# The first microseconds of an encoder kernel: x in column halves, the first weight tile in blocks

## The reference, cut to what matters

```python
def _rmsnorm(x, g):
    y = xf * lax.rsqrt(jnp.mean(xf * xf, axis=-1, keepdims=True) + RMS_EPS)
    return (y * g.astype(jnp.float32)).astype(x.dtype)

def _pool_mixer(h, w_in, w_group, scale, w_out):
    u = (h @ w_in).reshape(b, s, N_POOL_GROUPS, POOL_GROUP)      # h, w_in: 256x1024, 1024x1024
    ...                                                          # pooling, grouped product
    return y @ w_out

def reference(x, ...):
    for i in range(DEPTH):                    # DEPTH = 2
        hn = _rmsnorm(x, norm_mix[i])
        y = _pool_mixer(hn, ...)  if mixer == 0 else _dilated_mixer(hn, ...)
        x = x + y
        hn = _rmsnorm(x, norm_ffn[i])
        x = x + (_swiglu(hn, ...) if i % 2 == 0 else _moe(hn, ...))   # d_ff 3584; top 2 of 8 experts
    return _rmsnorm(x, norm_final)
```

## Time and profile before

| | |
|---|---|
| median of three runs | 1650.28 us |
| profiled execution, its own time | 1648.55 us |
| its span, first to last instruction | 1646.7 us |
| PE busy | 1595.2 us, 97% of the span |
| DVE, ACT busy | 1193.8 us (72%), 1006.1 us (61%) |
| chain that ended last | PE 93%, DVE 3%, issue 2%, ACT 1% |
| first matmul of the product starts | 15.41 us |
| first matmul with tile 1 starts | 21.08 us |

### The profile page before, as it was taken

How to read it: one execution, slowest core, us unless ns; L and a number is a source line. 1 busy time by engine, 2 the same in 40 slices (tenths; PEclk the granted TensorE clock), 3 DMA queues, 4 the chain that set the end, 5 groups by cost and what they waited for, 6 DMA issues and landing times.

```text
span 1646.7 us, 21670 instructions
## 1 busy us (share of the span) xinstructions
PE 1595.2 (97%) x7925; PEld 1311.0 (80%) x7925; DVE 1193.8 (72%) x977; ACT 1006.1 (61%) x815; POOL 130.3 (8%) x127
## 2 busy tenths in 40 slices
PE   8999999999899998999999999999999999995996
PEld 6888888899799876888888888888888888884885
DVE  4555454454654568888888888888888888984886
ACT  5444443433633466777777777777777777774774
POOL 0000000050332222000000000000000000000000
PEclk9999999999999999999999999999999999997998
DMA  9555555476266417999999999999999999997992
GB/s 344 187 181 180 192 182 184 154 240 196 77 188 221 154 53 268 360 375 356 372 377 353 375 374 353 375 371 356 376 372 355 370 378 355 376 345 252 364 360 86
DMA packets 237712, 468.87 MB, mean 285 GB/s; under 512 B 9632, under 2 KB 15776, under 8 KB 237648
## 3 DMA queue, kind: packets, MB, share of 16 engines
q1 hardware_dynamic: 231216, 454.06, 78.8%
q0 software_dynamic: 3024, 11.01, 2.2%
q10 hardware_dynamic: 3408, 2.93, 0.6%
HBM read 460.60 MB, written 7.37 MB: 284 GB/s over the span
## 4 chain that ended last, share of the span: by engine, by line
PE 93%; DVE 3%; issue 2%; ACT 1%; DMA 0%; SPq 0%; ACTq 0%; DVEq 0%
PE bY L291 9%; PE bY L293 9%; PE bY L292 9%; PE bU L291 8%; PE bG L291 8%; PE bU L293 8%; PE bU L292 8%; PE bG L292 8%; PE bG L293 8%; PE bS L293 3%; PE bS L292 3%; PE bS L291 3%; PE bT L530 2%; DVE logit L1238 1%; PE bT L293 1%
## 5 line engine op out<-in xcount | busy, mean ns | idle before, releaser
L281 DVE TENSOR_TENSOR wlo<-raw,whi 128x2048 fp32r<-128x2048 f32 x427 | 978.4, 2294 | 367.6 <-ACT whi L275 366.4
L275 ACT ACTIVATE whi<-raw 128x2048 fp32r<-128x2048 f32 x427 | 818.8, 1918 | 472.8 <-PE bY L293 163.7
L291 PE MATMUL bG<-whi,eTh 128*128 128x512 f32 x448 | 179.5, 401 | 16.9 <-issue 16.9
L291 PE MATMUL bU<-whi,eTh 128*128 128x512 f32 x448 | 182.9, 408 | 4.9 <-DVE wlo L281 4.9
L291 PE MATMUL bY<-whi,hTh 128*128 128x512 f32 x448 | 178.9, 399 | 0.0
L292 PE MATMUL bG<-whi,eTl 128*128 128x512 f32 x448 | 178.3, 398 | 0.0
L293 PE MATMUL bG<-wlo,eTh 128*128 128x512 f32 x448 | 178.2, 398 | 0.0
L292 PE MATMUL bU<-whi,eTl 128*128 128x512 f32 x448 | 178.1, 398 | 0.0
L293 PE MATMUL bU<-wlo,eTh 128*128 128x512 f32 x448 | 178.0, 397 | 0.0
L292 PE MATMUL bY<-whi,hTl 128*128 128x512 f32 x448 | 177.6, 396 | 0.0
L293 PE MATMUL bY<-wlo,hTh 128*128 128x512 f32 x448 | 177.5, 396 | 0.0
(11 more groups left out here) (404 smaller groups left out, 2333.9 us busy)
## 6 DMA issues: line engine op xcount, KB each, us to landing
raw<-in_m_w_gate_up_dram SPq DMA_DIRECT2D x224, 1024.0 KB, 6.4
raw<-in_m_w_down_dram SPq DMA_DIRECT2D x112, 1024.0 KB, 6.4
raw<-in_b_w_in_dram SPq DMA_DIRECT2D x36, 1024.0 KB, 5.2
raw<-in_f_w_gate_up_dram SPq DMA_DIRECT2D x28, 1024.0 KB, 5.2
raw<-in_f_w_down_dram SPq DMA_DIRECT2D x14, 1024.0 KB, 5.1
raw<-in_a_w_in_dram SPq DMA_DIRECT2D x4, 1024.0 KB, 11.2
raw<-in_a_w_out_dram SPq DMA_DIRECT2D x4, 1024.0 KB, 15.7
biasrev<-toeplitz SPq DMA_DIRECT2D x32, 128.0 KB, 4.9
```

The costliest lines, as they stand in the source:

```text
L275: nc.scalar.activation(whi[:, t % CUT], raw[:, t % RAW], ACT.Copy).then_inc(hi_done, 1)
L281: nc.vector.tensor_tensor(wlo[:, t % CUT], raw[:, t % RAW], whi[:, t % CUT].bitcast(F32), ALU.subtract).then_inc(lo_done, 1)
L291: pe.matmul(dst, a[0], b[0], start=start, stop=False)
```

## The change

x is loaded by halves of its columns: seven DMAs of 128 KB on SP and one on ACT's queue (`load_x`), with a semaphore for each half. The first weight tile is loaded as four DMAs of 128 rows (256 KB, a block each), between the two halves of x. ACT and DVE make its high and low parts block by block (128x512), with `first_hi` and `first_lo` counting. On PE 16 spare matmuls stand ahead of the transposes instead of 14, 6 behind instead of 15; the transposes of the second half of x stand between blocks 1 and 2 of tile 0; and tile 0 is worked by block (G and U in turn) instead of by bank. ACT and DVE make the high and low parts of tile 1 ahead of `xTh` and `xTl` of x's second half. ACT's table load waits for the zeroed tile instead of for the gains.

```diff
+        def load_x(engine, a, kh):
+            sl = slice(kh * 512, kh * 512 + 512)
+            engine.dma_start(x[a % 2 * 64:a % 2 * 64 + 64, a // 2, sl],
+                             x_in[0].rearrange("(m a) d -> a m d", a=4)[a][:, sl]).then_inc(x_in_done[kh], 16)
...
         @block.sync
         def _(sp):
+            for a in range(3):
+                load_x(sp, a, 0)
+            for b in range(4):
+                sp.dma_start(raw[:, 0, b * 512:b * 512 + 512],
+                             tile_source(0)[b * P:b * P + P, :]).then_inc(first_full[b], 16)
             for a in range(4):
-                sp.dma_start(x[a % 2 * 64:a % 2 * 64 + 64, a // 2, :],
-                             x_in[0].rearrange("(m a) d -> a m d", a=4)[a]).then_inc(x_in_done, 16)
+                load_x(sp, a, 1)
...
-            for t in range(T_MOE + CUT):
+            for t in range(1, T_MOE + CUT):
                 load(t)
...
             pe.wait_ge(spare_zero, 2)
-            spare(14, yTh[:, 0, 0:P], mixTh[:, 0:2])
+            spare(16, yTh[:, 0, 0:P], mixTh[:, 0:2])
             pe.wait_ge(c_in[C_IDENT], 16)
             turn_x(0, 0)
-            turn_x(0, 1)
-            spare(5, yTh[:, 0, 0:P], mixTh[:, 0:2])
-            spare(5, yTh[:, 1, P:2 * P], mixTh[:, 2:4])
-            spare(5, mixTh[:, 0, 0:P], mixTh[:, 2:4])
+            spare(6, yTh[:, 0, 0:P], mixTh[:, 0:2])
             pe.wait_ge(tx_lo, 2)
-            dense(T_IN, xTh, xTl, KH, (G, U), [lambda: pe.wait_ge(tx_lo, 4)])
+            for b in range(4):
+                pe.wait_ge(*((first_lo, b + 1) if b < 3 else (lo_done, 1)))
+                for tb, bank in enumerate((G, U)):
+                    mm = mm3(pe, bank[:], tok(xTh, xTl, b, tb), wblk(0, b), start=b == 0, stop=False)
+                if b == 1:
+                    turn_x(0, 1)
+            mm.then_inc(tile_used, 1)
+            pe.wait_ge(tx_lo, 4)
+            tile_ready(1)
...
             load_const((C_IDENT, C_GAINT))
+            load_x(act, 3, 0)
+            act.wait_ge(spare_zero, 2)
+            nc.scalar.activation(small[:, 8:9], yTh[:, 0, 0:1].bitcast(F32), ACT.Copy)
             act.wait_ge(c_in[C_IDENT], 16)
             act.wait_ge(c_in[C_GAINT], 16)
-            nc.scalar.activation(small[:, 8:9], gainT[:, 0, 0:1], ACT.Copy)
             cut_x(0, 0)
             load_const((C_BUCKET, C_RELB, C_SCALE))
-            make_hi(act, 0)
+            for b in range(4):
+                act.wait_ge(first_full[b], 16)
+                sl = slice(b * 512, b * 512 + 512)
+                nc.scalar.activation(whi[:, 0, sl], raw[:, 0, sl], ACT.Copy).then_inc(*((first_hi, 1) if b < 3 else (hi_done, 1)))
+            make_hi(act, 1)
             cut_x(0, 1)
-            for t in range(1, CUT):
-                make_hi(act, t)
+            make_hi(act, 2)
...
             cut_x(0, 0)
-            make_lo(dve, 0)
+            for b in range(4):
+                dve.wait_ge(*((first_hi, b + 1) if b < 3 else (hi_done, 1)))
+                sl = slice(b * 512, b * 512 + 512)
+                nc.vector.tensor_tensor(wlo[:, 0, sl], raw[:, 0, sl], whi[:, 0, sl].bitcast(F32),
+                                        ALU.subtract).then_inc(*((first_lo, 1) if b < 3 else (lo_done, 1)))
+            make_lo(dve, 1)
             cut_x(0, 1)
-            for t in range(1, CUT):
-                make_lo(dve, t)
+            make_lo(dve, 2)
```

More of the change, by code:

```diff
@@ L192, in encoder @@
         acc_dram = nc.dram_tensor("summed", (S + P, D), F32, kind="Internal").ap()
-        x_in_done = sem("x_in_done")
+        x_in_done = [sem("x_in_done0"), sem("x_in_done1")]
+        first_full, first_hi, first_lo = [sem(f"first_full{b}") for b in range(4)], sem("first_hi"), sem("first_lo")
         spare_zero = sem("spare_zero")
@@ L268, in tile_source @@
             return ffn_tile(m_w_gate_up[0, 0], m_w_down[0, 0], t - T_MOE)
+        def load_x(engine, a, kh):
+            sl = slice(kh * 512, kh * 512 + 512)
+            engine.dma_start(x[a % 2 * 64:a % 2 * 64 + 64, a // 2, sl],
+                             x_in[0].rearrange("(m a) d -> a m d", a=4)[a][:, sl]).then_inc(x_in_done[kh], 16)
         def make_hi(act, t, item=0):
-            act.wait_ge(raw_full[t % RAW], item * (16 * (FFN_TILES // RAW)) + 16 * (t // RAW + 1))
+            act.wait_ge(raw_full[t % RAW], item * (16 * (FFN_TILES // RAW)) + 16 * ((t - 1) // RAW + 1))
             if t >= CUT:
@@ L446, in turn_x @@
                 if n == 0:
-                    pe.wait_ge(x_in_done, 64)
+                    pe.wait_ge(x_in_done[kh], 64)
                 else:
@@ L482, in _ @@
             pe.wait_ge(spare_zero, 2)
-            spare(14, yTh[:, 0, 0:P], mixTh[:, 0:2])
+            spare(16, yTh[:, 0, 0:P], mixTh[:, 0:2])
             pe.wait_ge(c_in[C_IDENT], 16)
             turn_x(0, 0)
-            turn_x(0, 1)
-            spare(5, yTh[:, 0, 0:P], mixTh[:, 0:2])
-            spare(5, yTh[:, 1, P:2 * P], mixTh[:, 2:4])
-            spare(5, mixTh[:, 0, 0:P], mixTh[:, 2:4])
+            spare(6, yTh[:, 0, 0:P], mixTh[:, 0:2])
             pe.wait_ge(tx_lo, 2)
-            dense(T_IN, xTh, xTl, KH, (G, U), [lambda: pe.wait_ge(tx_lo, 4)])
+            for b in range(4):
[7 more added lines that the diff above has]
+            tile_ready(1)
+            for tb, bank in enumerate((G, U)):
+                for b in range(4):
+                    mm = mm3(pe, bank[:], tok(xTh, xTl, 4 + b, tb), wblk(1, b), start=False, stop=b == 3)
+            mm.then_inc(tile_used, 1)
             pe.wait_ge(c_in[C_BUCKET], 16)
@@ L842, in root @@
                 nc.scalar.activation(small[:, 9:10], ident[:, 0:1], ACT.Sqrt)
-                act.wait_ge(*((x_in_done, 64) if n == 0 else (x_final, 1) if n == 4 else (x_sum, (2, 4, 8)[n - 1])))
+                if n == 0:
+                    act.wait_ge(x_in_done[0], 64)
+                act.wait_ge(*((x_in_done[1], 64) if n == 0 else (x_final, 1) if n == 4 else (x_sum, (2, 4, 8)[n - 1])))
                 nc.scalar.activation((hn, squares)[n >= 3][:, 1], x[:, 1], ACT.Square, accum_out=ss[:, 1:2]).then_inc(sq_done, 1)
@@ L1125, in _ @@
             cut_x(0, 0)
-            make_lo(dve, 0)
+            for b in range(4):
+                dve.wait_ge(*((first_hi, b + 1) if b < 3 else (hi_done, 1)))
[3 more added lines that the diff above has]
+            make_lo(dve, 1)
             cut_x(0, 1)
-            for t in range(1, CUT):
-                make_lo(dve, t)
-            dve.wait_ge(x_in_done, 64)
+            make_lo(dve, 2)
+            dve.wait_ge(x_in_done[0], 64)
+            dve.wait_ge(x_in_done[1], 64)
             stats(0)
```

## The result

| | before | after |
|---|---|---|
| median | 1650.16 us (4 runs) | 1637.88 us (4 runs, 1636.55 to 1639.76) |
| profiled execution, its own time | 1648.55 us | 1637.73 us |
| span | 1646.7 us | 1635.9 us |
| first matmul of the product | 15.41 us | 12.22 us |
| first matmul with tile 1 | 21.08 us | 21.11 us |

The ratio is 0.9934, with a 95% interval of 0.9905 to 0.9963: 12.3 us faster, where 1.3 were forecast and 1646.8 was the lower end of the range. The last two rows of the table hold nearly all of it. The start, which the change is about, gave nothing. The gain lies 1500 us later, in code that the change does not touch.

The account below looks back on a forecast made before the run. PE, 93% of the last-ending chain, was taken as the bound, late at the start through tile 0's transfer. Tile 1 starting at 19.82 instead of 21.08 gives -1.26 us, so 1649.0 us against the median; range 1646.8 to 1651.9.

Parts of the forecast that it names:

- Behind it PE's work is the same list: After tile 1's start PE's work is unchanged, so the later of tile 0's end and tile 1's readiness, against 21.08, decides all.
- Lost on the way: Rival, chance 0.15: PE's late 16.95 us wait and low clock, 2 us, may return the gain or add; without gain 1650.3.
- Tile 1 lands at 13.87: At the start, tile 1's transfer lands as before, with the same 2 MB ahead; PE starts it at 19.82, 1.26 us earlier.
- tile 1 comes late: Rival, chance 0.14: SP's queue runs dry before tile 1's issue; gain gone if landing after 15.1, at 17.6 1652.7 us.
- Transposes at 7.9, first product matmul at 11.94: Start of PE's work: transposes 0.57 us earlier than 8.47, first product matmul at 11.94 instead of 15.41.
- Low clock, 0.06: Rival, chance 0.06: fewer spare matmuls and new idle times drop PE to 0.43 us a matmul in tile 0; 1652.3 us.
- The chain behind the landing and the cover behind it: From tile 1's landing at 13.87, ACT and DVE work until PE starts at 19.82; tile 3's low part keeps 3 us cover.
- Faster by over 0.2%: Chance 0.07 that the whole kernel gains more than 3.3 us; slower had 0.06, within 0.87.

Follow-up runs that it names:

- e1: The kernel before with seven spare matmuls fewer behind the transposes (8 instead of 15), nothing else; 1638.91 us against 1650.25, ratio 0.9929.
- e2: The changed kernel with seven spare matmuls more behind the first transposes (13 instead of 6); 1651.73 us, ratio 1.0009 against the kernel before.
- e3: The changed kernel with SP issuing tile 1 ahead of x's second half instead of behind it; 1636.47 us, ratio 0.9918 against the kernel before.

## Why the prediction was wrong, step by step

- *"Behind it PE's work is the same list", so that the start is the whole effect.* This step failed, and with it the size: what an edit to the list's length costs elsewhere stood in the sum at nothing. The work is the same, but the list is 14 instructions shorter, and the place of a loop in the list has a price: 11.1 us of PE's wait (e1 has it without the rest of the change, e2 takes it back and keeps the rest).
- *"Lost on the way."* I had the right row, but priced only its second half, the low clock, at 2 us, and took the 16.95 us of "issue" as given. The gain came from there and not from the start: that the forecast had the right sign is luck. The question that I should have put is what the sequencer does in 17 us in which no operand is awaited.
- *Tile 1 lands at 13.87.* It landed at 15.23, past the point 15.1 that I gave for the rival "tile 1 comes late", which is what happened: no gain at the start. The bytes ahead of it were the same, but they took longer. From 4 to 7 us the rate was higher than in the earlier trace rows, 284 GB/s for 221, and from 8 to 13 us lower, 296 for 390; over the whole of 4 to 13 us it was 300 for 320, 0.18 MB less:

```profile
4.00:7.00 3.00, 3.00 (x9) 2.34 (x8) 0.00 (x0) 0.00 (x0) 0.00 (x0) 1.00 1.01 284
8.00:13.00 5.00, 3.01 (x18) 2.30 (x17) 3.28 (x7) 3.76 (x8) 0.00 (x0) 1.00 1.04 296
```

  The DMA share is 1.01 and 1.04, so the engines were not idle: what stood in the queue moved slowly, and that was x's second half, 64 partitions at a time, right ahead of tile 1. In e3, where it stands behind tile 1, the slow stretch moves with it: 225 to 246 GB/s from 12 to 15 us, 338 to 377 from 9 to 12. But the kernel before has the same 1 MB of x in pieces of 64 partitions, so that alone is not the difference. The first 2 MB were through at about 12.0 (x's last piece was issued at 6.68 and took 5.3), where tile 0 ended at 11.0 before; that is 1.0 of the 1.4 us. What cost it, the smaller pieces, their order or their number, was not separated.
- *Transposes at 7.9, first product matmul at 11.94.* 7.80, and 12.22: right within 0.3. ACT's small issues ended at 10.68 instead of 10.31. Tile 0 was whole only at 10.2, not at 8.7 to 9, but ACT came to it no sooner than 10.72. A 128x512 block took 0.61 us on ACT and 0.68 on DVE, as taken.
- *Low clock, 0.06.* It came, for 3 us, and cost nothing (e2). The row that I put against it, an idle of 1.57 us without a fall, was one execution. The price of 0.43 us for a matmul was right, but its row was not: the profile has the clock of the first spare matmuls at 1.00. At a granted 0.50 the changed kernel's matmuls start 0.43 apart (14.22, 14.65).
- *The chain behind the landing and the cover behind it.* Right: 5.86 us for 5.95, and no wait for tile 3 or `rstd` on PE; the low part of tile 3 started at 27.08, 1.3 us later than thought, since everything behind tile 1's landing was.
- *Chances.* "Faster by over 0.2%" had 0.07. All cases but the last hung on the start, and none had a price for the jump.

Not explained: why the fetches come back at certain places of the tail. The traces show three packets more, not what makes them needed.

## What to carry to other kernels

Where a profile says that an engine waited for "issue" longer than a microsecond or two, look at its branches: the first jump over long code costs 6 us here, and jumping over it again next to nothing or 11 more, by where it happens to lie. The packets on the instruction queue tell which. An edit that changes the number of instructions ahead of such a loop must be compared with one that changes only that number, or its gain and loss are those of the place. One test around a loop that is usually empty leaves one jump of it, 6.1 to 6.3 us in each of the four kernels that had it, and is worth more here (15.2 us) than the whole work on the start. The four cover two places of the loop; that no place is bad for the outer test is not shown.

## What the runs showed of the hardware that I had not expected

PE's first jump over the 1215 instructions took 6.1 to 7.4 us in every kernel. The same jump when the loop goes round took 0.22 us or 11.5 us (11.41 to 11.58), two instructions of shift deciding it. The bad place came back at a shift of 256 and not at 128 or 242, which fits a period of 256 instructions; other shifts were not tried. From 730 to 1490 us, while PE goes through the loop over the experts again and again, no packet comes on its instruction queue at all, so the loop's instructions stay held meanwhile.

The Trainium skill (Runtime: NRT & Kernel Launch, "Instruction fetch mechanics") says that instructions are fetched by DMA in blocks of 16 KiB, 256 instructions, and that a taken branch to a target outside the current window of two blocks has to wait for such a fetch. The packets of 16 KB and their number in the long jumps agree. The window of two blocks does not: head and tail of this loop lie 1215 instructions, almost five blocks, apart, and the third jump took 0.22 us before and after the change.
